# RMS norm of a mixer's two latents: with tokens on partitions, in place of column sums and a spread on TensorE

## The reference, cut to what matters

```python
def rmsnorm(x, g):
    xf = x.astype(jnp.float32)
    y = xf * lax.rsqrt(jnp.mean(xf * xf, axis=-1, keepdims=True) + EPS)
    return (y * g.astype(jnp.float32)).astype(x.dtype)

z = h @ w_in                       # h: 256 x 1024
z_na, c_q, c_kv, k_rope, z_gq, z_gkv, z_gate = jnp.split(z, offs, axis=-1)
y_na = neighbourhood_attention(na_qkv ...)          # 8 heads of 64
q  = rmsnorm(c_q,  g_qa)  @ w_uq    # c_q:  256 x 384
kv = rmsnorm(c_kv, g_kva) @ w_ukv   # c_kv: 256 x 256
```

## Time and profile before

| what | value |
|---|---|
| median of 3 runs | 1663.76 us (1662.39 to 1665.04) |
| span of the profiled execution | 1666.6 us |
| mean granted TensorE clock | 0.985 |
| TensorE, VectorE, ScalarE busy | 96%, 67%, 55% |
| layer 0, s0 to `uqr` | 52.82 to 114.80 us |
| layer 1, s0 to `uqr` | 504.05 to 562.28 us |

### The profile page before, as it was taken

How to read it: one execution, slowest core, us unless ns; L and a number is a source line. 1 busy time by engine, 2 the same in 40 slices (tenths; PEclk the granted TensorE clock), 3 DMA queues, 4 the chain that set the end, 5 groups by cost and what they waited for, 6 DMA issues and landing times. The chain is left out here.

```text
span 1666.6 us, 29494 instructions
## 1 busy us (share of the span) xinstructions
PE 1601.8 (96%) x12268; PEld 1450.0 (87%) x12268; DVE 1113.0 (67%) x1750; ACT 918.3 (55%) x1471; POOL 302.4 (18%) x222
## 2 busy tenths in 40 slices
PE   7899999999999999999999998889999999899998
PEld 7898998999888999989998986768888889878886
DVE  4575656787466656568865687469945778779744
ACT  4656855666347567556654654236633566545531
POOL 0000120243000002104320352015500021008300
PEclk9899999999999999999999999899999999999999
DMA  7634454565664344555554632115565534345652
GB/s 222 183 109 149 139 181 161 193 211 172 209 168 148 134 138 140 203 177 178 198 190 168 230 115 91 41 60 194 197 222 189 200 128 152 127 154 180 242 186 72
DMA packets 45396, 272.95 MB, mean 164 GB/s; under 512 B 4816, under 2 KB 9040, under 8 KB 16208
## 3 DMA queue, kind: packets, MB, share of 16 engines
q1 hardware_dynamic: 44544, 266.36, 46.6%
q10 hardware_dynamic: 720, 4.72, 0.8%
HBM read 270.01 MB, written 1.05 MB: 163 GB/s over the span
## 5 line engine op out<-in xcount | busy, mean ns | idle before, releaser
L315 DVE TENSOR_TENSOR b_wlo<-b_wraw,b_whi 128x2048 fp32r<-128x2048 f32 (+1 forms) x264 | 571.7, 2169 | 201.8 <-PE b_ps L437 125.9
L307 ACT ACTIVATE b_whi<-b_wraw 128x2048 fp32r<-128x2048 f32 (+1 forms) x264 | 469.3, 1779 | 217.6 <-PE b_ps L437 147.7
L358 PE MATMUL b_ps<-b_H,b_whi 128*128 128x256 f32 x1784 | 506.9, 284 | 0.9 <-ACT b_four L846 0.9
L360 PE MATMUL b_ps<-b_H,b_whi 128*128 128x256 f32 x1784 | 498.8, 280 | 0.0
L361 PE MATMUL b_ps<-b_H,b_wlo 128*128 128x256 f32 x1784 | 498.7, 280 | 0.0
L358 PEld LDWEIGHTS b_ps<-b_H,b_whi 128*128 128x128 f32 x1784 | 336.3, 189 | 6.8 <-issue 4.9
L360 PEld LDWEIGHTS b_ps<-b_H,b_whi 128*128 128x128 f32 x1784 | 336.4, 189 | 0.7
L361 PEld LDWEIGHTS b_ps<-b_H,b_wlo 128*128 128x128 f32 x1784 | 336.0, 188 | 0.0
L404 PE MATMUL b_ps<-b_H,b_whi 128*128 128x512 f32 x448 | 155.7, 390 | 0.0
L1537 POOL TENSOR_TENSOR b_fl<-b_ab,b_fh 128x256 fp32r<-128x256 f32 x44 | 93.8, 2131 | 213.6 <-ACT b_fh L1510 213.6
L405 PE MATMUL b_ps<-b_H,b_wlo 128*128 128x256 f32 x448 | 126.3, 282 | 0.0
(11 more groups left out here) (360 smaller groups left out, 2729.5 us busy)
## 6 DMA issues: line engine op xcount, KB each, us to landing
b_wraw<-in_w SPq DMA_DIRECT2D x223, 1024.0 KB, 4.9
b_wraw<-in_w SPq DMA_DIRECT2D x37, 512.0 KB, 3.5
b_bias<-in_rpb SPq DMA_DIRECT2D x8, 512.0 KB, 11.5
b_gains<-in_gains ACTq DMA_DIRECT2D x4, 1024.0 KB, 4.9
b_wraw<-in_w SPq DMA_DIRECT2D x2, 768.0 KB, 4.3
b_cA<-in_cA SPq DMA_DIRECT2D x2, 576.0 KB, 8.9
b_X<-in_x SPq DMA_DIRECT2D x2, 512.0 KB, 5.4
out<-b_X SPq DMA_DIRECT2D x4, 256.0 KB, 2.5
```

Source lines behind the costliest of these rows:

```text
L307: e.activation(whi[u % NHI][:, 0:n], raw[u % NRAW][:, 0:n], ACT.Copy).then_inc(up("w_hi", "whi", u))
L315: e.tensor_tensor(wlo[u % NLO][:, 0:n], raw[u % NRAW][:, 0:n], hi.bitcast(F32), ALU.subtract).then_inc(up("w_lo", "wlo", u))
L358: e.matmul(out, wh, x.hi[:, kk, :], start=k == 0, stop=False)
L360: e.matmul(out, wh, x.lo[:, kk, :], start=False, stop=False)
```

## The change

`lat` becomes two jobs in row form, `cq` of 384 columns in two units of 4 row blocks (1536 wide) and `ck` of 256 columns in one unit (2048 wide). Their six blocks give tokens on partitions. ScalarE squares a finished block from PSUM and sums along the row in the same instruction; VectorE, after that sum, copies the block to `zl`. At the end of `ck` ScalarE takes both roots; at rot0 VectorE takes the reciprocals and scales the four blocks in place. A new step `latents` after rot1 transposes five 128-wide pieces for both token blocks (ten transposes into three banks), ScalarE writes the high parts with the gain, VectorE the low parts. Column sums, spreads and POOL's part go. Bank 7 joins the rings. The order becomes: s0 cq cq cq; s1 t0 cq v0 ck ck; s2 t1 rot0 v1 rot1 latents; s3 t2 rot2 v2 rot3 rot4; t3 rot5 v3; vg vg_turn.

```diff
...
-    def square_act(e, w, src):
...
-    def stat_pe(e, w, src, k, n, values):
...
-    def spread_pe(e, w, c, key, need):
...
-    def root_act(e, w, n):
...
-    def root_dve(e, w):
...
-    def rms_pe(e, w):
...
-    def rms_dve(e, w, src, n, gkey, lo, hi, key, keep=None):
...
-    def rms_act(e, w, n, hi, key, keep=None):
...
-    def rms_pool(e, w, n, lo, hi, key, keep=None):
...
-                    self.cq, self.ck = sb(s2, "cq", [P, 3, T]), sb(s2, "ck", [P, 2, T])
+                    self.zl = sb(s2, "zl", [P, 2, 640])
...
-            self.lat = Job(f"lat{l}", "w_in", l, range(8), pieces(1536, 2176), H)
+            self.lat = [Job(f"cq{l}", "w_in", l, range(8), [np.arange(1536, 1920)], H, per_unit=1, kpart=4),
+                        Job(f"ck{l}", "w_in", l, range(8), [np.arange(1920, 2176)], H, per_unit=1)]
...
-            fill = [("lat", j) for j in range(5)] + [("latk",)] + [("rot", j) for j in range(6)] + [("vg",), ("vg_turn",)]
+            fill = [("lat", c, pi, tb) for c in range(2) for _, pi, tb in row_blocks(self.lat[c])]
+            fill += [("rot", 0), ("rot", 1), ("latents",)] + [("rot", j) for j in range(2, 6)] + [("vg",), ("vg_turn",)]
...
+        LATENTS = [(0, (0, 1)), (0, (2,)), (1, (0, 1))]
+
+        def lat_ahead(self, e, w, split, ahead, c, pi, tb):
+            u = begun[(self.lat[c].key, 0)]
+            if c == 1 or (pi, tb) == (0, 0):
+                ahead_to(e, w, split, u[0] + ahead)
+            elif (pi, tb) == (1, 1):
+                ahead_to(e, w, split, u[1] + ahead)
+
+        def lat_rows(self, c, tb):
+            return self.zl[:, tb, 384 * c:384 + 256 * c]
+
+        def lat_sum_act(self, e, w, c, tb):
+            l, key = self.l, (self.lat[c].key, 0, tb)
+            n = w.next("spare")
+            if n:
+                w.wait_ge(*at("spare", n - 1))
+            w.wait_ge(*at("full", key))
+            width = len(self.lat[c].tiles[0])
+            e.activation(spare[:, 0:width], banks.tile(key)[:, 0:width], ACT.Square, accum_out=nst[:, 2 * c + tb:2 * c + tb + 1]).then_inc(up("sums", "spare", n))
+            sig.same(("lat_sum", l, c, tb), ("spare", n))
+
+        def lat_root_act(self, e, w):
+            l = self.l
+            for c in range(2):
+                for tb in range(2):
+                    w.wait_ge(*at("lat_sum", l, c, tb))
+                width = len(self.lat[c].tiles[0])
+                e.activation(nst[:, 4 + 2 * c:6 + 2 * c], nst[:, 2 * c:2 * c + 2], ACT.Sqrt, bias=eps_rms, scale=1.0 / width).then_inc(up("lat_root", "lat_root", l, c))
+
+        def lat_copy_dve(self, e, w, c, tb):
+            key = (self.lat[c].key, 0, tb)
+            w.wait_ge(*at("full", key))
+            w.wait_ge(*at("lat_sum", self.l, c, tb))
+            e.tensor_copy(self.lat_rows(c, tb), banks.tile(key)[:, 0:len(self.lat[c].tiles[0])]).then_inc(banks.free(key))
+
+        def lat_scale_dve(self, e, w):
+            l = self.l
+            w.wait_ge(*at("lat_root", l, 0))
+            w.wait_ge(*at("lat_root", l, 1))
+            e.reciprocal(nst[:, 8:12], nst[:, 4:8]).then_inc(up("lat_rinv", "lat_rinv", l))
+            w.wait_ge(*at("lat_rinv", l))
+            for c in range(2):
+                for tb in range(2):
+                    w.wait_ge(*at("free", (self.lat[c].key, 0, tb)))
+                    z = self.lat_rows(c, tb)
+                    e.tensor_scalar(z, z, nst[:, 8 + 2 * c + tb:9 + 2 * c + tb], None, ALU.mult).then_inc(up("lat_n", "lat_n", l, c, tb))
+
+        def latents_pe(self, e, w):
+            for n, (c, fs) in enumerate(self.LATENTS):
+                bank = banks.take(w, ("latents", self.l, n))
+                for tb in range(2):
+                    w.wait_ge(*at("lat_n", self.l, c, tb))
+                for g, f in enumerate(fs):
+                    for tb in range(2):
+                        ins = e.transpose(bank[:, g * T + tb * P:g * T + tb * P + P], self.lat_rows(c, tb)[:, f * P:f * P + P], ident)
+                ins.then_inc(banks.full(("latents", self.l, n)))
+
+        def latents_act(self, e, w):
+            for n, (c, fs) in enumerate(self.LATENTS):
+                x, gain = (self.cqs, "mla_qa_g") if c == 0 else (self.cks, "mla_kva_g")
+                w.wait_ge(*at("full", ("latents", self.l, n)))
+                for g, f in enumerate(fs):
+                    e.activation(x.hi[:, f, :], banks.tile(("latents", self.l, n))[:, g * T:g * T + T], ACT.Identity,
+                                 bias=zero, scale=par_col(f"{gain}{self.l}", f)).then_inc(up("h_hi", x.key, "hi", f))
+
+        def latents_dve(self, e, w):
+            for n, (c, fs) in enumerate(self.LATENTS):
+                x, gain, key = (self.cqs, "mla_qa_g", ("latents", self.l, n)) if c == 0 else (self.cks, "mla_kva_g", ("latents", self.l, n))
+                w.wait_ge(*at(x.key, "hi", fs[-1]))
+                for g, f in enumerate(fs):
+                    ins = e.scalar_tensor_tensor(x.lo[:, f, :], banks.tile(key)[:, g * T:g * T + T], par_col(f"{gain}{self.l}", f),
+                                                 x.hi[:, f, :].bitcast(F32), ALU.mult, ALU.subtract)
+                    if f != fs[-1]:
+                        ins.then_inc(up("h_lo", x.key, "lo", f))
+                    else:
+                        ins.then_inc(banks.free(key))
+                        sig.same((x.key, "lo", f), ("free", key))
...
-            banks.assign(lin=ALL, att=ALL)
+            banks.assign(lin=EVERY, att=EVERY)
...
                 tile_pe(e, w, self.k, j)
-            banks.assign(lin=SOME, att=ATT)
+            banks.assign(lin=SOME + [STAT], att=ATT)
             for what, *i in self.first:
                 if what in ("scores", "turns", "weights", "values"):
                     pair_pe(e, w, self.na, what, *i)
...
-                    j, = i
-                    tile_pe(e, w, self.lat, j)
-                    if j == 2:
-                        for k in range(3):
-                            stat_pe(e, w, self.cq[:, k, :], k, 3, False)
-                    if j == 3:
-                        rms_pe(e, w)
-                    if j == 4:
-                        stat_pe(e, w, self.ck[:, 0, :], 0, 2, False)
-                elif what == "latk":
-                    stat_pe(e, w, self.ck[:, 1, :], 1, 2, False)
+                    c, pi, tb = i
+                    row_pe(e, w, self.lat[c], 0, pi, tb)
+                elif what == "latents":
+                    self.latents_pe(e, w)
                 elif what == "rot":
-                    j, = i
-                    if j == 0:
-                        rms_pe(e, w)
-                    rot_pe(e, w, self.rot, j, self.tn)
+                    rot_pe(e, w, self.rot, *i, self.tn)
...
-                    j, = i
-                    ahead_act(e, w, self.lat, j)
-                    dst = self.cq[:, j, :] if j < 3 else self.ck[:, j - 3, :]
-                    w.wait_ge(*at("full", (self.lat.key, j)))
-                    e.activation(dst, banks.tile((self.lat.key, j))[:, 0:T], ACT.Copy).then_inc(banks.free((self.lat.key, j)))
-                    w.wait_ge(*at("free", (self.lat.key, j)))
-                    square_act(e, w, dst)
-                    if j == 2:
-                        root_act(e, w, 3)
-                    if j == 3:
-                        rms_act(e, w, 3, self.cqs.hi, self.cqs.key)
-                elif what == "latk":
-                    root_act(e, w, 2)
+                    c, pi, tb = i
+                    self.lat_ahead(e, w, split_hi, AHEAD_HI, *i)
+                    if pi == len(begun[(self.lat[c].key, 0)]) - 1:
+                        self.lat_sum_act(e, w, c, tb)
+                        if c == 1 and tb == 1:
+                            self.lat_root_act(e, w)
+                elif what == "latents":
+                    self.latents_act(e, w)
                 elif what == "rot":
-                    if i[0] == 0:
-                        rms_act(e, w, 2, self.cks.hi, self.cks.key)
...
-                    j, = i
-                    ahead_dve(e, w, self.lat, j)
-                    if j == 2:
-                        root_dve(e, w)
-                    if j == 3:
-                        rms_dve(e, w, self.cq, 3, f"mla_qa_g{l}", self.cqs.lo, self.cqs.hi, self.cqs.key)
-                elif what == "latk":
-                    root_dve(e, w)
+                    c, pi, tb = i
+                    self.lat_ahead(e, w, split_lo, AHEAD_LO, *i)
+                    if pi == len(begun[(self.lat[c].key, 0)]) - 1:
+                        self.lat_copy_dve(e, w, c, tb)
+                elif what == "latents":
+                    self.latents_dve(e, w)
                 elif what == "rot":
                     if i[0] == 0:
-                        rms_dve(e, w, self.ck, 2, f"mla_kva_g{l}", self.cks.lo, self.cks.hi, self.cks.key)
+                        self.lat_scale_dve(e, w)
...
-            rms_pool(e, w, 3, self.cqs.lo, self.cqs.hi, self.cqs.key)
```

(73 more changed lines are left out.)

3 lines of the change are left out of this document (1 added, 2 removed).

## The result

The changed kernel takes 1668.67 us (median of 20 runs, 1662.56 to 1673.24); in the same series the kernel before takes 1663.96 us (20 runs, 1658.77 to 1668.49). The ratio is 1.0029, with a 95% interval of 1.0018 to 1.004: about 4.8 us slower. Forecast was 1661.7 us, within 0.2% of before.

The account below looks back on a forecast made before the run. TensorE, 96% busy, was taken as the bound: 3.2 us gained in layer 0 and 1.9 in layer 1, less 3.0 for low clock, made 2.1 net, scaled to 1661.7 us. Range 1656.0 to 1668.0.

Parts of the forecast that it names:

- The chain: ScalarE and VectorE work from the third latent unit's split to pair 0's values (v0), put at 12.1 us.
- the two stretches: TensorE from pair 0's scores (s0) to the first uqr tile, per layer; 62.0 and 58.2 us before the change.
- Rival 2: No stall before v0, ScalarE and VectorE being early: gain 11.8 us, 1652.0 us; chance 0.12.
- Rival 5: Each of two table switches ahead of v1 costs twice 1.3 us: 3.3 us slower, 1667.1 us; chance 0.03.
- Net gain 2.1 us: Both layers' s0 to uqr: 5.1 us gained at full clock less 3.0 for low clock.
- so I leave it there: Layer 0: the third latent unit's transfer still ends at 57.95, as bytes up to that point are unchanged.
- The bound: Third unit's transfer later for its 0.5 MB more: 1.4 us of loss in each layer.
- is busy for most of that: At v2, TensorE works through most of the ten passes ahead of pair 3; only 0.3 us is added.
- a fall in each layer: TensorE's clock drops after the stall before v0, 3.4 us at half clock: 1.5 us lost per layer.
- Rival 1: Clock stays up in one or both layers: gain 3.6 to 5.1 us, 1658.7 to 1660.2 us; chance 0.23.
- Rival 3: Clock falls before v0 and stays low through the stall before v1: 4.9 us worse, 1668.7 us; chance 0.12.
- Rival 4: Stalls at v0, v1 and v2 take all of the 5.1 us gain: 1663.8 us; chance 0.08.

Follow-up runs that it names:

- second profile: The kernel before, unedited, profiled once more for one execution: 1660.13 us, stretches of 56.7 and 55.3 us.
- combined order: Changed kernel with copy before sum, sums and roots in one step behind the turn's copies, whole cq blocks in one slot, transposes behind rot5: 1659.65 us, ratio 0.9998.
- after three times: Three traces of the unaltered changed kernel: ratios to the kernel before 1.0029, 1.0033 and 1.0027.
- copy first: Changed kernel with VectorE copying the finished block at once and ScalarE squaring and summing the copy: 1666.22 us, ratio 1.001.
- seven banks: Changed kernel with the rings outside the first part given back their old seven banks: 1669.01 us, ratio 1.0037.
- latents late: Changed kernel with the step latents moved from behind rot1 to behind rot4: 1667.37 us, ratio 1.0029.
- no sums: Kernel before with squares, column sums, roots and spreads left out, VectorE multiplying by the gain alone: 1653.14 us, ratio 0.9938.
- the narrow one: Changed kernel with ck in two units of 1024 columns instead of one of 2048, later splits moved: 1663.42 us, ratio 1.001 in its first run.
- the second narrow run: Changed kernel with ck in two units of 1024, run again beside the changed kernel (1668.77) and before (1662.89): 1664.95 us, ratio 1.0007.
- the last kernel: Changed kernel with copy before sum, sums and roots together, transposes at the end of the first part, and ck in two units: 1658.21 us, ratio 0.9973.

## Why the prediction was wrong

**The chain held.** The price of every step from the third split to v0 was right, 12.4 us against 12.1, and the stalls it named came: 3.2 and 3.4 before v0 (foretold 3.5 and 3.2), 1.97 and 1.95 before v1 (foretold 1.9). The copy of the latents waits for the square as expected. No row of the new transposes has an idle time. Nothing outside the two stretches moved in this trace. Ahead of v0's stall the waits lay otherwise than foretold: turn 0 waits 1.21 and 0.35 us in layer 1 and not at all in layer 0, where 1.6 and 0.5 were foretold for layer 0 and none for layer 1, since it was layer 1 in which the third unit came late. Rival 2 (no stall at v0) is excluded by the trace. Rival 5 is too: table load at 78.10, root at 79.39, load at 79.89, exponential at 81.19,

```profile
78.10 1.28 ACT L1182 ACT_TABLE_LOAD   x1
79.39 0.48 ACT L1182 ACTIVATE b_nst<-b_nst,b_c 128x2 f32<-128x2 f32 x2
79.89 1.28 ACT L883 ACT_TABLE_LOAD   x1
81.19 0.51 ACT L883 ACTIVATE b_S<-b_S,b_small 128x256 f32<-128x256 f32 x1
```

each behind the other at once, so that a switch costs 1.3 us. The Trainium skill, ScalarE: Activation LUTs, "What ACT_TABLE_LOAD costs", has about 2.66 us with a drain; the trace of after disagrees with it as that of before did.

**The step that failed: "Net gain 2.1 us: the profiled execution's span 1666.6 becomes 1664.5", and its scaling to the median.** The new marks were worked out forward from the start of the third split, at full clock, and the gain was taken as their distance from the marks of one execution. Summed forward instead, the prediction's stretches are 62.0 + 58.2 - 2.1 = 118.1 us; with the 1546.4 outside and the 1.9 us by which a run's time exceeds its span (1669.51 against 1667.6) that gives 1666.4 us. But the execution of before with 120.2 us in the stretches was long: by the same sum it is 1668.5 us, 4.7 over the median of 1663.76. From the third split to v0 the old kernel took 19.3 and 17.9 us in that execution, with 13.4 us of low clock in its two stretches; in the second profile it took 17.7 and 16.6, with 3.4. The prediction booked all of the first pair as time that its own 12.1 us would replace. With the split times of the second profile (1.40 and 1.26) the same durations give 55.1 + 54.9 + 3.0 of clock = 112.9 us, against the 112.0 that it shows: the gain of 2.1 becomes a loss of 0.9. Going back from the medians of before, 1661.4 to 1664.0, its usual sum is by estimate 113 to 116. The remark "it stands 2.8 us over the median" compared a span with a run's time, and took the surplus off in proportion as if it lay in all the kernel. It lay in the two stretches under study. Counted from that execution, these 4.7 us are two thirds of the 7.0 by which the forecast missed; the rest is the 3.1 us between 118.1 and the 121.2 of after, less the 0.8 by which that execution is over its median. That the sum to an absolute time comes as near as 1666.4 is in part luck: the late splits of that execution, 5.13 and 2.76, stood in for the late arrival of the wide unit, which is the next step. Counted from the second profile the forecast would have been 1661.2, and by estimate most of the miss would fall to that step (2 x (3.5 - 1.3) = 4.4 us). Two profiles don't settle the share of each.

**The second: the arrival of the third unit, "so I leave it there".** In layer 1 of after the split starts 6.43 us after s0, and the prediction had 2.76; v0 comes at 18.84 in place of 14.85, 4.0 us later. The bound was there ("1.4 us of loss in each layer"), but was too small for layer 1 and was left out of the sum. Over the traces without the combined order the 2048 wide unit starts its split 3.5 us after s0 (mean of 12 layers: after three times, copy first, seven banks, latents late), the 1024 wide of before's kind 2.4 (6 layers, "no sums" among them, 0.6 to 5.1), the narrow one 0.9 (4 layers). The scatter is as large as the effect: in layer 0 after was 2.6 us earlier than foretold, and in the combined order wide and narrow start alike (1.7 and 2.8, 1.5 and 2.9). In the sum of both layers the third split and v0 alone make +4.0 - 2.3 = +1.7 us.

**The third: the size of v1 to `uqr`.** 28.0 foretold, 29.1 measured in each layer: the wait at v2 is 1.58 us and not 0.3. The prediction named the ten passes ahead of pair 3 and assumed that TensorE "is busy for most of that". Moved away, they give back 1.37 us. That is +2.2 in both layers.

**The clock.** The prediction took a fall in each layer, 1.5 us each. After has one, of 3.6 us in layer 0, behind the stall before v0, and none in layer 1 behind a longer stall (windows of TensorE: from and to, us, busy of each engine with its instructions, granted clock, share of DMA, GB/s):

```profile
69.00:75.00 6.00, 5.99 (x45) 5.67 (x46) 3.69 (x9) 4.44 (x6) 0.00 (x0) 0.72 0.26 87
521.60:525.00 3.40, 3.40 (x36) 3.23 (x37) 1.14 (x4) 3.40 (x5) 0.00 (x0) 1.00 0.52 157
```

The price was right: v0 to v1 is 15.36 us with the fall and 13.83 without, 1.5 us. Its count was one too high, so -1.5. Rival 1 had its sign in layer 1 (granted clock 1.00 behind v0), but its gain didn't come. Rival 3 gave nearly the time that was measured (1668.7), but not by its mechanism, as no low stretch is longer than 3.7 us in the three traces of this kernel; that it hit the number is luck. Rival 4 is nearest in kind, stalls at v0, v1 and v2 that take the gain; they took more than it.

**The sum.** Against the 118.1 foretold: +1.7 (arrival), +2.2 (v2), -1.5 (clock), +0.6 (v0 to v1, 0.3 in each layer): 121.1, and the trace has 121.2. The chances had "slower" at 0.15, the range ended 0.7 us under the result. The loss as against before comes from the stalls that ScalarE's and VectorE's chain puts before v0, v1 and v2: with them shortened the loss is gone. By single edits it is the wide unit on a chain that had no slack (3.8 of 5.9 us, by the second narrow run), then the copy behind the sum (3.3 us, intervals overlapping) and the passes ahead of pair 3 (2.7 us, by the trace alone). These overlap and are no sum. All edits of the last kernel together, the new order of steps among them, are worth about 10 us, 1668.77 to 1658.21.

**Open.** Why the transfer arrives at a different time in each execution was not tried. What the narrow unit gains by its earlier arrival, by two splits shorter by 0.9 us each and by the split that moves behind v0 was not told apart. Nor was another way of taking the roots tried, which could free the 2.6 us of table loads ahead of v1; the 2.16 us there stay.

## What to carry to other kernels

When new marks are worked out from durations, sum them to an absolute time and set that against the median; don't subtract them from the marks of one execution, unless a second profile shows the same marks. Ask first whether the profiled execution's surplus over the median lies in the stretch that is changed. When sums move from TensorE to the engine that releases it, look at that engine's chain from the transfer on: the width of a unit that the chain must wait for, an order that makes one engine's copy follow another's sum, and a batch of passes ahead of the next masks cost 2.7 to 3.8 us each here, where some 7 us were to be had.
